# Expert weights in six places of 2 MiB, with neighbouring rows in each partition

## The chip, the cores and the metric

The kernel runs on one core of a Trainium2 chip. The metric is the device time of one execution in microseconds; lower is better. Engines are named as in the profile: PE is TensorE, DVE VectorE, ACT ScalarE, POOL GpSimd and SP SyncE, which here only issues DMAs.

## The reference

One layer of a hybrid decoder over 256 prompt tokens and 8 sample tokens. A token mixer (Mamba-2 branch, attention branch, output product) is followed by a layer norm, a mixture of 32 experts of which each token takes four, and a second norm. All weights are float32. The change concerns the experts alone:

```python
def run_block(args):
    tok_b, g_b, e = args
    h = xpad[tok_b] @ w_gate_up[e] + b_gate_up[e]        # 1024 -> 2048
    gate, up = h[:, :D_FF], h[:, D_FF:]
    gate = jnp.minimum(gate, SWIGLU_LIMIT)
    up = jnp.clip(up, -SWIGLU_LIMIT, SWIGLU_LIMIT)
    hmid = (up + 1.0) * (gate * jax.nn.sigmoid(SWIGLU_ALPHA * gate))
    out = hmid @ w_down[e] + b_down[e]                   # 1024 -> 1024
    return out * g_b[:, None].astype(out.dtype)
```

Every expert has 8 MiB of gate-up weights (1024 rows of 2048 floats, 8 KB a row) and 4 MiB of down weights (1024 rows of 1024 floats, 4 KB a row), 384 MiB for the 32.

## The kernel before

Up to about 460 us the token mixer runs; w_out follows until about 505 us, then the router, which ends at about 520 us. The expert stage takes the rest. It goes block by block, a block being up to 64 rows that go to one expert. With these inputs there are 32 blocks, one for each expert.

The order of a block on PE is written out by hand in the loop at L2097: gate_up(b) (L2035), down(b-1) (L2047), gather(b+1) (L2024), combine(b-1) (L2069), gate_rows(b) (L2062). Gather takes the block's rows of x1 with one-hot columns. Gate_up multiplies them, as the stationary operand in tiles of 128x32, with the weights as the moving operand: four matmuls of 512 columns (q = 0 to 3) run at the same time in four column groups of the array, and each of them goes through the array twice since the data is float32. DVE turns the result in blocks of 32x32 (L1545), adds the bias, clips, and makes hst (L1564), the stationary operand of down in the block after. Down has its result in bank 2 in two halves that run at the same time.

Weights come by DMAs of SP, 1 MiB each. A gate-up chunk is 128 neighbouring rows, one row of 8 KB in each partition (L468): partition p holds row p of the chunk. A down chunk is 256 rows, two of them of 4 KB in each partition, 128 rows apart (L472). The chunks rotate through 12 places (moe_slot, L330), made of tensors that earlier stages have left: whm, wmh, wmx and five of wnat; chunk 0 has a place of its own that is used once (EARLY). PE increments chunk_used after each chunk, and SP waits for the release of a place before it issues the next load into it: 20 loads are written out at L478 to L494, then block_chunks (L496) makes 12 a block, eight of gate-up and four of down of the block before. So SP's queue is always limited by releases, and as many chunks as are free are in flight. Of these 20, the ninth waits for branch_b (its place holds w_out_attn), the tenth to twelfth for one release of w_out each, the thirteenth for mix_psum. Behind that wait SP also issues the last six pieces of the copy of the key and value caches (move_cache, L364, DRAM to DRAM, about 1 MB each).

The places of columns matter for the change. The moving operand of gate-up is read as `w[:, q, u, k, i]` of columns (u k q i), 32 neighbouring floats at a time (L2040). Gather reads x1 as (k q i) in the same way (L2030).

## Time and profile before

| | |
|---|---|
| Time, median of three runs | 1500.97 us (1499.21 to 1502.39) |
| The profiled execution's own time | 1498.68 us |
| Its span, first to last instruction | 1497.0 us |
| PE busy | 1351.9 us (90%) |
| DVE, ACT, POOL busy | 596.1, 298.1, 164.8 us |
| DMA moved | 539.26 MB, mean 360 GB/s |

The profile is of one execution. Times in it are counted from the span's start. Busy time of PE is modelled for the ends of matmuls, and matmuls overlap. A timeline row can merge several instructions (x8 at its end says how many), so its duration is from the first start to the last end. The share of the DMA engines can stand a little above 1, since packets overlap.

### The profile page before, as it was taken

How to read it: one execution, taken by the hardware profiler on the slowest of the kernel's cores; microseconds unless marked ns; L12 is line 12 of the kernel's file. 1: busy time of each engine (PE TensorE's matmuls, PEld its weight loads, DVE VectorE, ACT ScalarE, POOL GpSimd, SP SyncE). 2: the span in 40 equal slices, each digit the busy share in tenths (PEclk: the TensorE clock that was granted, in tenths of full speed). 3: DMA queues.
4: the chain of work that ended last, by engine and by line, in shares of the span. 5: the costliest groups of instructions: out<-in, count | busy, mean ns of one | idle time of the engine just before them, and what ended most of it. 6: DMA issues, size and time to landing. Idle time of an engine off the chain costs nothing.

```text
span 1497.0 us, 25740 instructions
## 1 busy us (share of the span) xinstructions
PE 1351.9 (90%) x10344; PEld 675.9 (45%) x10344; DVE 596.1 (40%) x899; ACT 298.1 (20%) x603; POOL 164.8 (11%) x219
## 2 busy tenths in 40 slices
PE   5998997988999799999999999999998999899984
PEld 4997887986675433333222222223222322232221
DVE  2886999967544523222212121222122212221224
ACT  3677654454130100000000000000000000000002
POOL 0004455230300000000000000000000000000002
PEclk9999998998799899999999999999999999999998
DMA  6699999969468989999999999999999999999993
GB/s 192 196 365 322 297 326 327 326 225 326 151 234 324 328 329 419 417 416 419 419 417 416 419 418 418 416 418 418 418 416 418 418 419 415 418 418 419 416 416 120
DMA packets 164655, 539.26 MB, mean 360 GB/s; under 512 B 11036, under 2 KB 90236, under 8 KB 130996
## 3 DMA queue, kind: packets, MB, share of 16 engines
q1 hardware_dynamic: 152768, 523.57, 90.0%
q10 hardware_dynamic: 10692, 10.91, 2.6%
q0 software_dynamic: 1152, 4.20, 0.8%
q8 instruction: 29, 0.48, 0.1%
q14 instruction: 14, 0.11, 0.0%
HBM read 522.39 MB, written 60.43 MB: 389 GB/s over the span
## 4 chain that ended last, share of the span: by engine, by line
PE 34%; SPq 28%; DMA 22%; DVE 8%; issue 5%; ACT 2%; POOL 1%; ACTq 0%; DVEq 0%; POOLq 0%
SPq L472 17%; DMA wmx<-in_w_down_dram 12%; SPq L468 11%; DMA wmh<-in_w_down_dram 9%; PE psum L2043 6%; PE psum L1813 4%; PE psum L2058 4%; PE psum L1632 3%; PE psum L1633 3%; PE psum L1634 3%; PE psum L1951 2%; DVE wlow L1052 2%; PE psum L2031 1%; PE psum L2077 1%; DMA gn_rows<-in_ssm_norm_g_dram 1%
## 5 line engine op out<-in xcount | busy, mean ns | idle before, releaser
L2043 PE MATMUL psum<-wnat,xst 128*32 128x512 f32 x2480 | 272.5, 593 | 0.4 <-DVE xst L1511 0.4
L1545 DVE STREAM_TRANSPOSE hturn<-psum 128x1024 f32<-128x1024 f32 x32 | 40.0, 1250 | 404.6 <-PE psum L2043 404.6
L1632 PE MATMUL psum<-xh,wh 128*128 128x264 f32 x592 | 177.6, 300 | 6.3 <-DVE wlow L1052 5.3
L1634 PE MATMUL psum<-xh,wlow 128*128 128x264 f32 x592 | 171.3, 289 | 0.0
L1633 PE MATMUL psum<-xl,wh 128*128 128x264 f32 x592 | 171.3, 289 | 0.0
L2043 PEld LDWEIGHTS psum<-wnat,xst 128*32 128x32 f32 x2480 | 77.5, 110 | 172.6 <-issue 172.6
L2058 PE MATMUL psum<-wmx,hst 128*64 128x512 f32 x496 | 118.7, 603 | 31.9 <-DMA wmx<-in_w_down_dram 31.9
L2058 PE MATMUL psum<-wmh,hst 128*64 128x512 f32 x496 | 119.0, 602 | 30.0 <-DMA wmh<-in_w_down_dram 30.0
L992 ACT ACTIVATE sg<-hb 128x512 f32<-128x512 f32 x32 | 20.2, 631 | 526.5 <-DVE hb L1553 526.5
L1632 PEld LDWEIGHTS psum<-xh,wh 128*128 128x128 f32 x592 | 115.8, 196 | 9.4 <-issue 6.3
L2043 PE MATMUL psum<-wmh,xst 128*32 128x512 f32 x1056 | 119.2, 592 | 0.0
L1052 DVE TENSOR_TENSOR wlow<-wraw,wh 128x1024 fp32r<-128x1024 f32 x74 | 109.3, 1492 | 21.6 <-ACT wh L688 21.6
L1633 PEld LDWEIGHTS psum<-xl,wh 128*128 128x128 f32 x592 | 115.6, 195 | 1.7 <-issue 1.7
L1634 PEld LDWEIGHTS psum<-xh,wlow 128*128 128x128 f32 x592 | 115.0, 194 | 0.0
L628 POOL COPY gcol<-gm 128x3 f32 (+1 forms) x32 | 17.0, 533 | 849.3 <-DVE hb L1548 848.3
L2031 PE MATMUL psum<-x,oneh 128*32 128x256 f32 x1584 | 93.8, 386 | 3.1 <-DVE oneh L1495 3.1
L1564 DVE TENSOR_TENSOR hst<-hu,sg 128x512 f32<-128x512 f32 x32 | 22.1, 692 | 160.3 <-PE psum L2058 160.3
L2058 PEld LDWEIGHTS psum<-wmh,hst 128*64 128x64 f32 x496 | 32.8, 136 | 116.7 <-issue 79.9
L2058 PEld LDWEIGHTS psum<-wmx,hst 128*64 128x64 f32 x496 | 31.0, 136 | 118.8 <-DMA wmx<-in_w_down_dram 78.2
L688 ACT ACTIVATE wh<-wraw 128x1024 fp32r<-128x1024 f32 x74 | 77.7, 1052 | 0.0
L2031 PEld LDWEIGHTS psum<-x,oneh 128*32 128x32 f32 x1584 | 48.5, 111 | 58.6 <-issue 27.6
L1813 PE MATMUL psum<-zz,wnat 128*128 128x264 f32 x256 | 69.6, 431 | 3.5 <-DVE gates L1299 3.5
(390 smaller groups left out, 1477.7 us busy)
## 6 DMA issues: line engine op xcount, KB each, us to landing
wnat<-in_w_gate_up_dram SPq DMA_DIRECT2D x155, 1024.0 KB, 20.1
wmh<-in_w_gate_up_dram SPq DMA_DIRECT2D x66, 1024.0 KB, 24.1
wmh<-in_w_down_dram SPq DMA_DIRECT2D x62, 1024.0 KB, 26.2
wmx<-in_w_down_dram SPq DMA_DIRECT2D x62, 1024.0 KB, 23.3
wraw<-in_w_in_dram SPq DMA_DIRECT2D x37, 1024.0 KB, 8.9
whm<-in_w_gate_up_dram SPq DMA_DIRECT2D x33, 1024.0 KB, 22.3
out_dram<-in_cache_kv_w_dram SPq DMA_DIRECT2D x32, 1023.5 KB, 8.6
out_dram<-hs SPq DMA_DIRECT2D x8, 1024.0 KB, 11.9
```

The costliest lines, as they stand in the source:

```text
L468: sp.dma_start(moe_slot(m), wgu[bass.ds(e, 1), k * P:(k + 1) * P, :].rearrange("a p n -> p (a n)")).then_inc(moe_sem(m), 16)
L472: sp.dma_start(moe_slot(m).rearrange("p (a n) -> p a n", a=2), wdn[bass.ds(e, 1), j * 256:(j + 1) * 256, :].rearrange("e (a p) n -> p (e a ...
L688: a.activation(high_of(m), half_of(wraw, m), ACT.Copy).then_inc(S("high_done"), 1)
L1052: v.tensor_tensor(half_of(wlow, m), half_of(wraw, m), high_of(m).bitcast(F32), ALU.subtract).then_inc(S("low_done"), 1)
L1545: v.transpose(hturn[:, :], psum[:, 0:2, :].rearrange("p h c -> p (h c)")).then_inc(S("hidden_out"), 1)
L1632: mm(out, hi[:, k, :], xh[:, k, :], start=(k == 0), stop=False)
L1633: mm(out, hi[:, k, :], xl[:, k, :], start=False, stop=False)
L1634: last = mm(out, lo[:, k, :], xh[:, k, :], start=False, stop=(k == KT - 1))
L1813: last = mm(bank[6 + odd][:, 0:T], w[:, k, odd * P:(odd + 1) * P], zz[:, KT * (r // 2) + k, :], start=(r == 0 and k == 0), stop=(r == 3 an ...
L2031: last = mm(bank[0][q * QW:(q + 1) * QW, 256 * h:256 * h + 256], oneh[:, t, h * QW:(h + 1) * QW], src, start=(t == 0), stop=(t == 2))
L2043: last = mm(bank[h][q * QW:(q + 1) * QW, :], xst[:, h, k, :], w[:, q, :, :, :], start=(k == 0), stop=(k == GU_CH - 1))
L2058: last = mm(bank[2][BLK * half:BLK * half + BLK, :], hst[:, k, :, :].rearrange("p h r -> p (h r)"), w[:, col:col + 512], start=(k == 0), s ...
```

## The change

Chunks are 2 MiB, and there are six places of 2 MiB in the same tensors; the fifth place of wnat and the place of chunk 0 that was used once are joined or left. GU_CH is 4 and DN_CH 2, so a block has six chunks (PAIR). In a gate-up chunk partition p now holds the two neighbouring rows 2p and 2p+1 of 256 (16 KB), in a down chunk the four rows 4p to 4p+3 of 512 (16 KB).

Since the rows of the product lie otherwise over the partitions, the contraction's order changes in three other places to match: gather reads every second float of x1 (L2030), gate-up takes its columns with a step of four floats (L2040), so that the hidden values come out in the order in which down's rows lie, and the turn of the bias rows reads every fourth (L1611). Counts of chunk_used that others wait for are halved. The six cache copies stand before the fifth load instead of the thirteenth, and the last down chunk comes as two DMAs of 1 MiB with semaphores of their own (moe_last), of which each has 8 KB in a partition.

```diff
--- before.py
+++ after.py
@@ -53,9 +53,9 @@
 N_PROJ = 37
 N_SSM, N_ATT, N_OUT = 8, 1, 4
 HSN = 2
-GU_CH, DN_CH = 8, 4
-SLOTS = 12
-EARLY = 1
+GU_CH, DN_CH = 4, 2
+SLOTS = 6
+PAIR = GU_CH + DN_CH
 NQ, QW = 4, 32
 
 
@@ -329,30 +329,20 @@
 
         def moe_slot(m):
 
-            if m < EARLY:
-                return whm[:, 0, :]
-            at = (m - EARLY) % SLOTS
-            if at == 0:
-                return whm[:, 1, :]
-            if at < 5:
-                return wmh[:, at - 1, :]
-            if at < 7:
-                return wmx[:, at - 5, :]
-            return wnat[:, at - 7, :]
+            at = m % SLOTS
+            two = (whm[:, 0:2, :], wmh[:, 0:2, :], wmh[:, 2:4, :], wmx[:, :, :], wnat[:, 0:2, :], wnat[:, 2:4, :])[at]
+            return two.rearrange("p a n -> p (a n)")
 
         def moe_sem(m):
-            return S(f"moe_first{m}") if m < EARLY else S(f"moe_in{(m - EARLY) % SLOTS}")
+            return S(f"moe_in{m % SLOTS}")
 
         def moe_landed(eng, m, rep=0):
 
-            if m < EARLY:
-                eng.wait_ge(moe_sem(m), 16)
-            else:
-                eng.wait_ge(moe_sem(m), 16 * ((m - EARLY) // SLOTS + 1) + 16 * rep)
+            eng.wait_ge(moe_sem(m), 16 * (m // SLOTS + 1) + 16 * rep)
 
         def gate_up_done(eng, b):
 
-            eng.wait_ge(S("chunk_used"), 8 if isinstance(b, int) and b == 0 else 12 * b + 4)
+            eng.wait_ge(S("chunk_used"), GU_CH if isinstance(b, int) and b == 0 else PAIR * b + 2)
 
         block = keep.enter_context(nc.Block())
 
@@ -464,42 +454,42 @@
                 native(i)
                 move_cache(next(pieces))
 
-            def gate_up(m, e, k):
-                sp.dma_start(moe_slot(m), wgu[bass.ds(e, 1), k * P:(k + 1) * P, :].rearrange("a p n -> p (a n)")).then_inc(
-                    moe_sem(m), 16)
+            def gate_up(m, e, j):
+
+                sp.dma_start(moe_slot(m), wgu[bass.ds(e, 1), j * 256:(j + 1) * 256, :].rearrange(
+                    "e (p a) n -> p (e a n)", a=2)).then_inc(moe_sem(m), 16)
 
             def down(m, e, j):
-                sp.dma_start(moe_slot(m).rearrange("p (a n) -> p a n", a=2),
-                             wdn[bass.ds(e, 1), j * 256:(j + 1) * 256, :].rearrange("e (a p) n -> p (e a) n", p=P)).then_inc(
-                    moe_sem(m), 16)
+
+                sp.dma_start(moe_slot(m), wdn[bass.ds(e, 1), j * 512:(j + 1) * 512, :].rearrange(
+                    "e (p a) n -> p (e a n)", a=4)).then_inc(moe_sem(m), 16)
 
             sp.wait_ge(S("oT_ready"), 3)
             sp.wait_ge(S("kv_out"), 16 * 12)
-            for m in range(20):
-                if m == 8:
-                    sp.wait_ge(S("branch_b"), KT // 2)
-                elif 9 <= m < 12:
-                    sp.wait_ge(S("native_used"), N_SSM + m - 8)
-                elif m == 12:
-                    sp.wait_ge(S("mix_psum"), 3)
+            for m in range(10):
+                if m == 4:
                     for piece in pieces:
                         move_cache(piece)
-                elif m > 12:
+                    sp.wait_ge(S("branch_b"), KT // 2)
+                    sp.wait_ge(S("native_used"), N_SSM + 1)
+                elif m == 5:
+                    sp.wait_ge(S("native_used"), N_SSM + 3)
+                elif m > 5:
                     sp.wait_ge(S("chunk_used"), m - SLOTS + 1)
-                if m < 8:
+                if m < 4:
                     gate_up(m, 0, m)
-                elif m < 16:
-                    gate_up(m, 1, m - 8)
+                elif m < 8:
+                    gate_up(m, 1, m - 4)
                 else:
-                    down(m, 0, m - 16)
+                    down(m, 0, m - 8)
 
             def block_chunks(b, e, e_before):
-                for c in range(12):
-                    sp.wait_ge(S("chunk_used"), 12 * b + c - 15)
+                for c in range(PAIR):
+                    sp.wait_ge(S("chunk_used"), PAIR * b + c - 7)
                     if c < GU_CH:
-                        gate_up(c + 8, e, c)
+                        gate_up(c + 4, e, c)
                     else:
-                        down(c + 8, e_before, c - GU_CH)
+                        down(c + 4, e_before, c - GU_CH)
 
 
             with sp.Fori(2, NE) as b:
@@ -515,9 +505,13 @@
                     block_chunks(b, e, before)
             last = sp.value_load(tab[0:1, bass.ds(nblk - 1, 1)], min_val=0, max_val=NE - 1)
             extra = sp.value_load(tab[0:1, MAX_BLK + 4:MAX_BLK + 5], min_val=0, max_val=MAX_OV)
-            for j in range(DN_CH):
-                sp.wait_ge(S("chunk_used"), 12 * extra + 12 * NE + j - 15)
-                down(j + 8, last, j)
+            sp.wait_ge(S("chunk_used"), PAIR * extra + PAIR * NE - 7)
+            down(4, last, 0)
+            sp.wait_ge(S("chunk_used"), PAIR * extra + PAIR * NE - 6)
+            quarter = moe_slot(5).rearrange("p (a n) -> p a n", a=4)
+            for i in range(2):
+                sp.dma_start(quarter[:, 2 * i:2 * i + 2, :], wdn[bass.ds(last, 1), 512:1024, :].rearrange(
+                    "e (p a) n -> p (e a) n", a=4)[:, 2 * i:2 * i + 2, :]).then_inc(S(f"moe_last{i}"), 16)
             for t in range(2):
                 for half in range(2):
                     cols = slice(512 * half, 512 * half + 512)
@@ -994,7 +988,7 @@
 
             def expert_rows(b):
 
-                act.wait_ge(S("chunk_used"), 12 * b + 20)
+                act.wait_ge(S("chunk_used"), PAIR * b + 10)
                 a.activation(orow[:, :], bank[2], ACT.Copy).then_inc(S("orow_ready"), 1)
 
             def gate_rows(b):
@@ -1010,7 +1004,7 @@
                 sigmoid(b)
                 expert_rows(b - 1)
                 gate_rows(b)
-            act.wait_ge(S("chunk_used"), 12 * nblk)
+            act.wait_ge(S("chunk_used"), PAIR * nblk)
             a.activation(orow[:, :], bank[2], ACT.Copy).then_inc(S("orow_ready"), 1)
 
 
@@ -1576,7 +1570,7 @@
                 gated(b)
                 one_hot(b + 1)
                 hidden(b)
-                dve.wait_ge(S("chunk_used"), 12 * b + 8)
+                dve.wait_ge(S("chunk_used"), PAIR * b + 4)
                 hidden_in(b)
                 rows_in(b + 1)
 
@@ -1608,7 +1602,9 @@
                 i, o = divmod(f, 12)
                 tr(bank[i][:, 32 * o:32 * o + 29], rows[:, f * P:(f + 1) * P], ident[0:29, 0:29])
             for f in range(2 * KT):
-                tr(bank[2][:, NE * f:NE * f + NE], bgu_rows[:, f * P:(f + 1) * P], ident[0:NE, 0:NE])
+                u, j, c = f // KT, f % KT // 4, f % 4
+                of_four = bgu_rows[:, :].rearrange("e (u j i c) -> e u j c i", u=2, j=2, c=4)
+                tr(bank[2][:, NE * f:NE * f + NE], of_four[:, u, j, c, :], ident[0:NE, 0:NE])
             tr(bank[3][:, 0:ZT], gn_rows[:, :], ident[0:ZT, 0:ZT]).then_inc(stage("params_psum"), 1)
 
             pe.wait_ge(S("x_in"), 32)
@@ -2027,7 +2023,7 @@
                 for h in range(2):
                     for t in range(3):
                         for q in range(NQ):
-                            src = x1[:, t, :].rearrange("p (k q i) -> p q k i", q=NQ, i=QW)[:, q, :, :]
+                            src = x1[:, t, :].rearrange("p (j q i a) -> p q j a i", q=NQ, i=QW, a=2)[:, q, :, :, :]
                             last = mm(bank[0][q * QW:(q + 1) * QW, 256 * h:256 * h + 256], oneh[:, t, h * QW:(h + 1) * QW],
                                       src, start=(t == 0), stop=(t == 2))
                 last.then_inc(S("gath_done"), 1)
@@ -2035,26 +2031,32 @@
             def gate_up(b, m0, rep):
 
                 pe.wait_ge(S("xst_ready"), b + 1)
-                for k in range(GU_CH):
-                    moe_landed(pe, m0 + k, rep)
-                    w = moe_slot(m0 + k).rearrange("p (u k q i) -> p q u k i", u=2, q=NQ, i=QW)
-                    for h in range(2):
-                        for q in range(NQ):
-                            last = mm(bank[h][q * QW:(q + 1) * QW, :], xst[:, h, k, :], w[:, q, :, :, :], start=(k == 0),
-                                      stop=(k == GU_CH - 1))
+                for j in range(GU_CH):
+                    moe_landed(pe, m0 + j, rep)
+                    w = moe_slot(m0 + j).rearrange("p (a u j q i c) -> p a q u j c i", a=2, u=2, j=2, q=NQ, i=QW)
+                    for a_ in range(2):
+                        k = 2 * j + a_
+                        for h in range(2):
+                            for q in range(NQ):
+                                last = mm(bank[h][q * QW:(q + 1) * QW, :], xst[:, h, k, :], w[:, a_, q, :, :, :, :],
+                                          start=(k == 0), stop=(k == KT - 1))
                     last.then_inc(S("chunk_used"), 1)
 
-            def down(b, m0, rep):
+            def down(b, m0, rep, final=False):
 
                 pe.wait_ge(S("hst_ready"), b + 1)
                 pe.wait_ge(S("gt_ready"), b + 1)
                 for j in range(DN_CH):
-                    moe_landed(pe, m0 + j, rep)
+                    in_halves = final and j == DN_CH - 1
+                    if not in_halves:
+                        moe_landed(pe, m0 + j, rep)
                     w = moe_slot(m0 + j)
-                    for a_ in range(2):
-                        k = 2 * j + a_
+                    for c in range(4):
+                        if in_halves and c % 2 == 0:
+                            pe.wait_ge(S(f"moe_last{c // 2}"), 16)
+                        k = 4 * j + c
                         for half in range(2):
-                            col = a_ * D + 512 * half
+                            col = c * D + 512 * half
                             last = mm(bank[2][BLK * half:BLK * half + BLK, :], hst[:, k, :, :].rearrange("p h r -> p (h r)"),
                                       w[:, col:col + 512], start=(k == 0), stop=(k == KT - 1))
                     last.then_inc(S("chunk_used"), 1)
@@ -2095,13 +2097,13 @@
             gather(1)
             gate_rows(0)
             with pe.Fori(1, nblk) as b:
-                gate_up(b, 8, b - 1)
-                down(b - 1, 16, b - 1)
+                gate_up(b, 4, b - 1)
+                down(b - 1, 8, b - 1)
                 pe.wait_ge(S("hidden_out"), b + 1)
                 gather(b + 1)
                 combine(b - 1, False)
                 gate_rows(b)
-            down(nblk - 1, 8, nblk - 1)
+            down(nblk - 1, 4, nblk - 1, final=True)
             combine(nblk - 1, True)
```

## Rows read from the trace of the kernel before

**Rows 1.** The page: DMA share and rate in 40 slices.

```profile
DMA  6699999969468989999999999999999999999993
GB/s 192 196 365 322 297 326 327 326 225 326 151 234 324 328 329 419 417 416 419 419 417 416 419 418 418 416 418 418 418 416 418 418 419 415 418 418 419 416 416 120
```

**Rows 2.** SP's issues in order of time (start us, us, queue, line).

```profile
698.10 1.03 SPq L468 DMA_DIRECT2D whm<-in_w_gate_up_dram  x1
...
1421.23 1.02 SPq L468 DMA_DIRECT2D whm<-in_w_gate_up_dram  x1
```

**Rows 3.** The same view, first issues of two early blocks.

```profile
551.32 7.18 SPq L468 DMA_DIRECT2D wnat<-in_w_gate_up_dram  x5
...
578.33 7.19 SPq L468 DMA_DIRECT2D wnat<-in_w_gate_up_dram  x5
```

**Rows 4.** One block in order of time; idle before in brackets.

```profile
999.97 1.94 PE L2058 MATMUL psum<-wmh,hst 128*64 128x512 f32 x8 [0.63 <-DMA wmh<-in_w_down_dram]
...
1007.54 1.94 PE L2058 MATMUL psum<-wmx,hst 128*64 128x512 f32 x8 [0.60 <-DMA wmx<-in_w_down_dram]
1009.41 2.80 PE L2031 MATMUL psum<-x,oneh 128*32 128x256 f32 x48
...
1015.53 8.79 PE L2043 MATMUL psum<-wnat,xst 128*32 128x512 f32 x80
...
1021.14 0.13 PEld L2043 LDWEIGHTS psum<-wnat,xst 128*32 128x32 f32 x4 [0.30 <-issue]
1021.57 0.13 PEld L2043 LDWEIGHTS psum<-wnat,xst 128*32 128x32 f32 x4 [0.30 <-issue]
...
1029.54 1.25 DVE L1545 STREAM_TRANSPOSE hturn<-psum 128x1024 f32<-128x1024 f32 x1 [12.72 <-PE psum L2043]
```

**Rows 5.** DMA view of windows 1028:1034, 1008:1024 and 1038:1054 us.

```profile
DMA packets 637, 2.45 MB, mean 408 GB/s; under 512 B 39, under 2 KB 39, under 8 KB 637
...
DMA packets 928, 6.75 MB, mean 422 GB/s; under 512 B 104, under 2 KB 104, under 8 KB 104
...
DMA packets 924, 6.72 MB, mean 420 GB/s; under 512 B 104, under 2 KB 104, under 8 KB 104
```

**Rows 6.** First blocks, and one window (PE, PEld, DVE, ACT, POOL, clock, DMA).

```profile
526.01 3.64 PE L2043 MATMUL psum<-whm,xst 128*32 128x512 f32 x32 [0.41 <-DVE xst L1511]
...
539.88 3.69 PE L2017 MATMUL psum<-bdn,gmT 32*128 32x512 f32 x8
...
549.19 8.79 PE L2043 MATMUL psum<-wnat,xst 128*32 128x512 f32 x80 [0.45 <-DVE xst L1511]
...
550.00:552.50 2.50, 2.50 (x28) 0.81 (x24) 0.00 (x0) 0.00 (x0) 0.00 (x0) 1.00 0.25 64
```

**Rows 7.** The end in order of time.

```profile
1459.46 1.94 PE L2058 MATMUL psum<-wmx,hst 128*64 128x512 f32 x8 [0.61 <-DMA wmx<-in_w_down_dram]
...
1461.33 2.80 PE L2031 MATMUL psum<-x,oneh 128*32 128x256 f32 x48
...
1468.42 7.09 PE L2058 MATMUL psum<-wnat,hst 128*64 128x512 f32 x32 [0.90 <-ACT gsam L1005]
```

**Rows 8.** Bias rows turned, and the issue of six cache copies.

```profile
15.94 1.89 PE L1611 MATMUL psum<-ident,bgu_rows 32*128 32x32 f32 x16
...
504.37 3.72 SPq L373 DMA_DIRECT2D out_dram<-in_cache_kv_w_dram  x6
```

**Rows 9.** Five DVE lines: count, min/median/max ns, first and last start.

```profile
L1502 DVE TENSOR_TENSOR pick<-pick,gate x1: 557/557/557, 521.3 to 521.3; 128x384 f32<-128x384 f32 x1
...
L1506 DVE TENSOR_REDUCE gm<-pick x1: 834/834/834, 521.9 to 521.9; 128x96 f32<-128x384 f32 x1
...
L1464 DVE TENSOR_REDUCE mask<-pick x3: 363/369/375, 511.6 to 515.3; 128x32 f32<-128x128 f32 x2, 8x32 f32<-8x128 f32 x1
...
L1263 DVE TENSOR_REDUCE ast<-pa x12: 285/286/287, 346.2 to 371.6; 128x1 f32<-128x128 f32 x12
...
L1264 DVE TENSOR_REDUCE ast<-pa x12: 407/408/409, 346.4 to 371.8; 128x1 f32<-128x256 f32 x12
```

## The prediction

> **What bounds the kernel now.** I read the page first, then the DMA's own view in short windows, then the order of time of one expert block, of the first blocks and of the end. [rows 1] is the page: in the 16th slice and after (about 561 us) the sixteen DMA engines are busy in every slice at 415 to 420 GB/s, and in the table above TensorE is busy nine tenths of the span. Both look like the bound, so the pace of each is needed by itself. [rows 2] gives the pace at which weights arrive: SP's issue of the same place falls at 698.10 and, 24 blocks later, at 1421.23, so a block takes 723.13 / 24 = 30.13 us. A block is 12 MiB, so 2.511 us a MiB. [rows 3] gives TensorE's own pace: at 551 and 578 us all places are full, TensorE waits for nothing, and SP's issues (each follows a release by TensorE) lie 27.01 us apart. TensorE therefore has 30.13 - 27.01 = 3.12 us of slack in a block. [rows 4] shows where it lies: in one block the first and the fourth down chunk start at 999.97 and 1007.54, so 2.52 us lie between two of them, and each is held up 0.6 us by its DMA; the gate-up run from 1015.53 to about 1029.3 is one piece of 13.7 us. The stage is bound by the arrival of weights, and everything that shortens a transfer counts about 30 times.
>
> **Packet size.** In [rows 5] the first window holds almost only packets of 4 KB (the down chunks, rows of 1024 floats; the count under 8 KB is all of it) and moves 408 GB/s; the other two hold packets of 8 KB (gate-up, rows of 2048 floats) and move 422 and 420. The small packets counted there are the completions. The same two places of other blocks spread by 2 GB/s about their means, and I take 410 and 422 GB/s: 1.0486 MB takes 2.557 and 2.485 us. Doubling the packet from 4 to 8 KB saved 0.072 us a MiB. If the cost is one fixed amount for each packet, going on to 16 KB halves the remaining count and saves half of that again, 0.036: 2.449 us a MiB, 428 GB/s. A block of six places then takes 12 x 2.449 = 29.39 us instead of 30.13. Bounds: nothing gained beyond 8 KB gives 2.485 (29.82 a block, the down chunks still gain); no packet cost at all left would be 2.485 - 0.072 = 2.413 (28.96 a block). I take the middle value, since a fixed cost a packet is the simplest reading of the two kinds of window.
> The Trainium skill (DMA: Bandwidth & Descriptors, Why small descriptors are slow) says that each packet has a fixed overhead of about 3 cycles, and (Bandwidth, Measured) that a 16 MB transfer ran at 425 GB/s. By the latter a block would take 29.6 us, close to the sum. The trace agrees in sign: 410 against 422.
>
> **How many blocks it counts for.** In [rows 6] TensorE starts gate-up of block 0 at 526.01, ends it at 539.88, and is back at 549.19. By then it has released 8 MiB, 12 more are loaded, and the DMA runs dry: share 0.25 at 550.0 to 552.5. It resumes after the first release (SP's issue at 551.32) with 20 of 384 MiB loaded. The last four are needed only by the very last down. So 384 - 20 - 4 = 360 MiB stand between the restart and the chunk that lets the tail begin: 360 x (2.511 - 2.449) = 22.3 us gained, bounds 9.4 (2.485) and 35.3 (2.413).
>
> **Coarser places, at the restart.** A place of 2 MiB is released after 3.43 us of matmuls instead of 1.71 (13.7 us for eight chunks, [rows 4]). The DMA is dry at that moment, so the restart is 1.7 us later. The four places released in block 0 are issued from 529.5 on and take 4.9 us each after some 2 us of latency, so the last of them lands at about 551.1, just before the new first release at 549.19 + 3.43 = 552.6: as many MiB are loaded as before. Cost 1.7 us.
>
> **Coarser places, in a steady block.** After the last down chunk of 2 MiB lands (call it 0), TensorE needs 3.55 us for it, 6.05 for gather, combine and gate rows (1009.48 to 1015.53, [rows 4]) and 13.75 for gate-up: 23.4, with 0.6 before the next down. The next gate-up places land at 4.9, 9.8, 14.7 and 19.6, each before it is wanted; the down places at 24.5 and 29.4. The first is done at 28.1, 1.3 us before the second lands. Nothing is lost, with 1.3 us of cover within a block and 29.39 - 27.01 = 2.4 us over it. The queue doesn't run dry either: the unread backlog at the start of gate-up is at most 10 us of transfer, two places, one more is being read, so at least three of six are in flight. TensorE starts 12 MiB (29 us) behind and gains 2.4 us a block, so it has caught up after some twelve of 31 blocks.
>
> **Coarser places, at the end.** In [rows 7] the last down chunk of the loop starts at 1459.46, right after landing, and what follows never waits for a transfer: gather at 1461.33, down of the last block from 1468.42 for 7.09 us, then the norm and the outputs to 1497. With 2 MiB the same run of down takes 3.5 us after its landing instead of 1.9: 1.6 us later. The split of the very last place into two halves buys nothing here, since TensorE reaches it about 3 us after both have landed; it costs nothing either.
>
> **The cache copies.** The six copies left over, now issued behind mix_psum at 504.37 in 3.72 us ([rows 8]), move ahead of the fifth place on SP. Places 5 and 6 queue behind them. They wait for the first and third release of w_out and so are issued before 504.4, when the last one lets the copies go today. Six copies and 4 MiB take under 30 us together, and the places are wanted only at 549. Nothing on SP behind them is due earlier. The very first places are issued at 464 to 468.6 as before. What of SP's waits goes (half of them) was no cost: SP waits for releases. Cost 0, covered by some 15 us or more; without that cover the copies would cost their own time, about 12 us (six times 1 MB read and written at 420 GB/s and twice that at most). The permuted bias transposes read their stationary operand with a step; the 16 of them span 1.9 us ([rows 8]), so even doubled they cost 1.9 us. I take 0.
>
> **The step in the moving operand.** Now the matmuls of gate-up read weights in runs of 32 neighbouring floats; afterwards every fourth float (16 bytes apart), and gather every second of x1. No TensorE row of before has such an operand, so this is bounded. Low end 0. The nearest rows are VectorE's [rows 9]: 384 floats in runs take 557 ns (L1502), a reduction that reads 384 floats with a step of 32 takes 834 (L1506), 1.50 times; between 128 and 384 stepped floats the slope is (834 - 369) / 256 = 1.82 ns, against (408 - 286) / 128 = 0.95 in runs (L1263, L1264): 1.9 times. Applied to the 13.75 us of gate-up that is 6.9 or 12.6 us a block. I take 0, because TensorE takes 512 columns in 0.43 us, 0.83 ns for a float of one stream ([rows 4], four streams at once), already only a little faster than VectorE's 0.95, and its pace is set by float32 arithmetic in two passes and not by the first access; this is the weakest step.
>
> **Sum.** Span 1497.0 - 22.3 + 1.7 + 1.6 = 1478.0. The profiled execution took 1498.68, 1.7 over its span and 2.3 under the median of the three runs, 1500.97. On the median: 1500.97 - 19.0 = 1482.
>
> **Rivals.**
> (a) Larger packets bring nothing beyond 8 KB: 1500.97 - 9.4 + 3.3 = 1494.9. For it: two kinds of packet are all that the trace shows. Against: the gain from 4 to 8 KB is plain. Chance 0.10.
> (b) Slower: the step in the weights slows gate-up. It decides from 2.4 us a block, 17% of gate-up's time; below 1.3 it costs nothing. At 1.50 times a block is 27.0 + 6.9 = 33.9 us of TensorE: block 0 ends at 549.2 + 6.9 = 556.1, 31 blocks to 1607, tail 29.5, 1636 of span, about 1640. At 1.9 times it is 39.6 a block, about 1823. For it: [rows 9], and that four streams share the reading side at once, where they could hurt each other more than one. Against: nothing in the trace but the pace above. Chance 0.20 for a slowdown of this kind. The Trainium skill (SBUF — State Buffer, Door 1, on cachelines) has the rule behind it: lines are 16 bytes, at least two accesses must fall in one for full rate, and four float32 are as far as a step is free. Here each line would give one float. By [rows 9] VectorE agrees; no TensorE row can say.
> (c) A small slowdown, 2.4 to 3.2 us a block, from gather's step of two or the same cause: TensorE is the bound at 29.4 to 30.2 us and the time is within some 3 us of the present. Chance 0.05.
> (d) Six places are too few: with one read and one partly filled the DMA idles 0.3 to 1 us a block. 30 x that: 1491 to 1512. Against: the backlog worked out above leaves three in flight. Chance 0.05, most of it slower.
>
> **How the numbers follow.** Forecast 0.60; (a) 0.10, (b) 0.20, (c) 0.05, (d) 0.05. 0.2% is 3 us, about what a measurement of this kernel can tell from no change. Faster: 0.60 + 0.10 = 0.70; same: (c) and a part of (d), 0.07; slower: 0.23. The range leaves out (b) and reaches from near the best packet price (1469, taken as 1472) to the end of (d), 1512.
>
> **What would show it.** Windows of packets of 16 KB at about 428 GB/s, the same place issued every 29.4 us; gate-up still one run of 13.7 us and gather 2.8; TensorE waiting for DMA only ahead of down; a DMA share of 1 from about 557 on; the tail from the last down of the loop 1.6 us longer. Wrong if gate-up's run is over 16 us, or if rows of TensorE show no waits for DMA late in the stage: then (b) or (c). Wrong the other way if the windows still show 422.

## The result, and the profile after

| | before | after |
|---|---|---|
| Time, median (lowest to highest) | 1500.82 us (1499.21 to 1502.39) | 1915.24 us (1910.46 to 1917.26) |
| Span of the profiled execution | 1497.0 us | 1914.9 us |

The change makes the kernel slower by the factor 1.2757, with a 95% interval of 1.2728 to 1.2785. The forecast was 1482 with a range of 1472 to 1512. The time lies far outside it, on the side of rival (b).

The page of after, the parts that answer to [rows 1], with PE's busy time, the chain and the costliest line, and below them the chain of before:

```profile
PE 1824.9 (95%) x10344; PEld 707.5 (37%) x10344; DVE 595.5 (31%) x899; ACT 298.0 (16%) x603; POOL 164.5 (9%) x219
...
DMA  6899997767746777777867777787777778777770
GB/s 193 295 339 311 331 323 260 242 231 285 281 176 264 281 296 299 301 292 312 314 270 303 291 293 300 303 314 299 274 299 303 293 292 314 313 278 293 292 291 23
...
PE 90%; DVE 5%; issue 2%; ACT 1%; DMA 1%; POOL 1%; another core or an unknown queue 1%; ACTq 0%; DVEq 0%; POOLq 0%
...
L2041 PE MATMUL psum<-wnat,xst 128*32 128x512 f32 x1984 | 453.6, 1081 | 0.5 <-DVE xst L1505 0.5
```

```profile
PE 34%; SPq 28%; DMA 22%; DVE 8%; issue 5%; ACT 2%; POOL 1%; ACTq 0%; DVEq 0%; POOLq 0%
```

In the expert stage the DMA engines now have seven to eight tenths of their time busy and move about 300 GB/s where 415 to 420 stood. The chain of work that ended last, followed back from the end, is now nine tenths PE; before, half of it was SP's queue and its transfers. A gate-up matmul takes 1081 ns where the page of before has 593, and the granted clock is 1.00 from 600 to 1880 us, so it is not the clock. So the stage has changed its bound: before it waited for weights, now the weights wait.

One block of after in order of time, which answers to [rows 4], then two passes of gate-up's weight loads, then SP's issue of the same place in two blocks, which answers to [rows 2]:

```profile
1026.16 3.65 PE L2060 MATMUL psum<-wmh,hst 128*64 128x512 f32 x16
1029.65 3.60 PE L2060 MATMUL psum<-wmx,hst 128*64 128x512 f32 x16
1033.18 2.94 PE L2027 MATMUL psum<-x,oneh 128*32 128x256 f32 x48
...
1039.45 14.68 PE L2041 MATMUL psum<-wnat,xst 128*32 128x512 f32 x64
...
1068.51 1.94 PE L2060 MATMUL psum<-wmh,hst 128*64 128x512 f32 x8
```

```profile
1044.84 0.15 PEld L2041 LDWEIGHTS psum<-wnat,xst 128*32 128x32 f32 x4 [0.75 <-issue]
1045.74 0.15 PEld L2041 LDWEIGHTS psum<-wnat,xst 128*32 128x32 f32 x4 [0.75 <-issue]
```

```profile
1019.22 0.33 SPq L459 DMA_DIRECT2D whm<-in_w_gate_up_dram  x1
...
1061.52 0.33 SPq L459 DMA_DIRECT2D whm<-in_w_gate_up_dram  x1
```

No row has a wait for a DMA in its brackets. Gate-up runs from 1039.45 to the first down matmul at 1068.51, 29.1 us instead of 13.75; a pass of four matmuls takes 0.90 us instead of 0.43 [rows 4]. Down and combine are as they were. A block takes 42.30 us, and that is 27.01 [rows 3] + 32 passes x 0.47 = 15.04 + 0.14 for gather (2.94 instead of 2.80) = 42.19.

The span grew by 417.9 us. Block 0 starts at 530.90 instead of 526.01: 4.9. From there to the second block's gate-up (574.31) it is 43.41 us instead of 23.18: 20.2, of which gate-up is 15.3 and a lower clock behind it 4.8 (run 6). From the second block to the start of the last block's down (1886.36; before 1468.42, [rows 7]) it is 1312.05 instead of 919.23 us, 31 blocks of 42.3: 392.8. The tail after that is as long as before (28.5 and 28.6).

The first 4.9 us have a cause of their own, which the row of PE's one new wait names:

```profile
511.71 0.66 PE L1964 MATMUL psum<-xres,wr 128*32 128x128 f32 x8 [10.95 <-DMA bdn<-in_b_down_dram]
```

The router's logits wait 10.95 us for a load of 128 KB on ACT's queue, the experts' down bias. It lands 53.7 us after its issue, in the kernel before 27.0. From the end of w_out to block 0 it is 30.2 us here and 21.7 before, 8.5 more; the start moved by 4.9 only because w_out ended 3.6 us earlier in this execution (500.69 against 504.27).

### The profile page after: what moved, and what is told of

Same layout as the page of the kernel before. It is cut to its first block, busy times and chain, and to the rows that moved or that the text cites. A ratio compares the mean times of both kernels' runs of the same rounds, so it can differ in the third digit from the quotient of the medians.

```text
span 1914.9 us, 25006 instructions
## 1 busy us (share of the span) xinstructions
PE 1824.9 (95%) x10344; PEld 707.5 (37%) x10344; DVE 595.5 (31%) x899; ACT 298.0 (16%) x603; POOL 164.5 (9%) x219
## 4 chain that ended last, share of the span: by engine, by line
PE 90%; DVE 5%; issue 2%; ACT 1%; DMA 1%; POOL 1%; another core or an unknown queue 1%; ACTq 0%; DVEq 0%; POOLq 0%
PE psum L2041 48%; PE psum L2060 12%; PE psum L2027 5%; PE psum L1809 3%; PE psum L2079 3%; PE psum L1628 3%; PE psum L1629 3%; PE psum L1630 3%; PE psum L2084 2%; PE psum L1947 1%; DVE wlow L1046 1%; PE psum L2068 1%; DMA wnat<-in_w_out_dram 0%; DMA gn_rows<-in_ssm_norm_g_dram 0%
## 5 line engine op out<-in xcount | busy, mean ns | idle before, releaser
L2041 PE MATMUL psum<-wnat,xst 128*32 128x512 f32 x1984 | 453.6, 1081 | 0.5 <-DVE xst L1505 0.5
L2041 PE MATMUL psum<-wmh,xst 128*32 128x512 f32 x1056 | 245.3, 1083 | 0.0
L2041 PE MATMUL psum<-whm,xst 128*32 128x512 f32 x1024 | 237.4, 1080 | 0.4 <-DVE xst L1505 0.4
L2041 PEld LDWEIGHTS psum<-wnat,xst 128*32 128x32 f32 x1984 | 71.8, 126 | 329.9 <-issue 329.9
L986 ACT ACTIVATE sg<-hb 128x512 f32<-128x512 f32 x32 | 20.2, 631 | 1010.9 <-DVE hb L1547 1010.9
L2041 PEld LDWEIGHTS psum<-wmh,xst 128*32 128x32 f32 x1056 | 41.8, 129 | 196.7 <-issue 196.7
L2060 PE MATMUL psum<-wmh,hst 128*64 128x512 f32 x496 | 113.3, 599 | 0.0
L2060 PE MATMUL psum<-wmx,hst 128*64 128x512 f32 x496 | 111.7, 592 | 0.0
L2041 PEld LDWEIGHTS psum<-whm,xst 128*32 128x32 f32 x1024 | 41.2, 129 | 188.6 <-issue 188.1
L2027 PE MATMUL psum<-x,oneh 128*32 128x256 f32 x1584 | 101.2, 404 | 3.1 <-DVE oneh L1489 3.1
```

The source lines that it names most:

```text
L2027: last = mm(bank[0][q * QW:(q + 1) * QW, 256 * h:256 * h + 256], oneh[:, t, h * QW:(h + 1) * QW], src, start=(t == 0), stop=(t == 2))
L2041: last = mm(bank[h][q * QW:(q + 1) * QW, :], xst[:, h, k, :], w[:, a_, q, :, :, :, :], start=(k == 0), stop=(k == KT - 1))
L2060: last = mm(bank[2][BLK * half:BLK * half + BLK, :], hst[:, k, :, :].rearrange("p h r -> p (h r)"), w[:, col:col + 512], start=(k == 0), s ...
```

## The experiments

Three questions: is it the step of four in gate-up, and nothing else (runs 1 and 2)? What in the step costs (3 and 4)? What is the rest of the change worth (5 to 11)? The kernel before ran beside them on each chip, at 1496.5 to 1497.1 us.

**1. The step of four alone, in the kernel before.**

```diff
-  w = moe_slot(m0 + k).rearrange("p (u k q i) -> p q u k i", u=2, q=NQ, i=QW)
+  w = moe_slot(m0 + k).rearrange("p (u j q i c) -> p q u j c i", u=2, j=2, q=NQ, i=QW)
```

> The kernel before with one part of the change alone: gate-up reads its moving operand with a step of four floats; loads, places, copies and gather stay. The hidden values then stand in another order than the rows of down, so the experts' output is another one. Theory: gate-up takes 32 passes of 0.90 us, 28.8 instead of 13.7 us, TensorE is the bound at 27.0 + 15.1 = 42.1 us a block, 549.2 + 15.1 + 31 x 42.1 + 29.5 gives a span of about 1899, near 1900 us. Rival: the slowdown needs the transfers of 16 KB beside it; then the time stays near 1497 us.

Measured 1900.76 us, ratio 1.2696 (1.266 to 1.2732). SP's issues of one place, eight blocks apart:

```profile
797.91 0.33 SPq L468 DMA_DIRECT2D whm<-in_w_gate_up_dram  x1
...
1134.49 0.33 SPq L468 DMA_DIRECT2D whm<-in_w_gate_up_dram  x1
```

336.58 / 8 = 42.07 us a block. This one line carries 404 of the 414 us. The rest of the change, which was to save 19 us, costs some here: the span of after is 15.6 us longer than that of this run (1914.9 against 1899.3), since block 0 starts 8.7 us later and each of 31 blocks takes 0.23 us more, of which gather's step of two is 0.14. Cheaper transfers bring nothing while PE is the bound.

**2. All of the change without that step.**

```diff
-  w = moe_slot(m0 + j).rearrange("p (a u j q i c) -> p a q u j c i", a=2, u=2, j=2, q=NQ, i=QW)
+  w = moe_slot(m0 + j).rearrange("p (a u k q i) -> p a q u k i", a=2, u=2, q=NQ, i=QW)
```

> The changed kernel with one thing undone: gate-up reads its moving operand in runs of 32 neighbouring floats again. The hidden values then stand in another order than the rows of down, so the experts' output is another one; loads, places, gather with its step of two and every count of instructions are those of the changed kernel. Theory: the step of four floats in gate-up's moving operand is the whole loss, and the rest of the change does what the prediction said. Then four matmuls take 0.43 us again instead of 0.90, a block is bound by its transfers at 29.4 us, and the time is 1482 us (1475 to 1490). Rival 1: the coarse places or gather's step lose too; then a block takes over 30 us and the time is above 1500. Rival 2: matmuls are slow since the transfers of 16 KB disturb the reading side; then 0.90 us stays and the time is near 1915.

Measured 1487.0 us, ratio 0.9936 (0.9915 to 0.9956). SP's issues of the place whm, 23 blocks apart:

```profile
731.97 0.33 SPq L459 DMA_DIRECT2D whm<-in_w_gate_up_dram  x1
...
1408.15 0.33 SPq L459 DMA_DIRECT2D whm<-in_w_gate_up_dram  x1
```

676.18 / 23 = 29.40 us a block, where the prediction had worked out 29.39. The kernel before beside it had 1496.47, so it gains 9.5 us where the prediction's sum had 19.0 for all but the step. The wait at the logits is here too (9.8 us), and runs 7 to 11 are about it.

**3. Eight patterns of the moving operand in one gate-up.** In the kernel before, each of the eight chunks is read in another way; all matmuls have 512 columns.

```diff
+  if k == 0:
+      return flat[:, 512 * q:512 * q + 512]
+  if k == 1:
+      return flat[:, 128 * q:128 * q + 1024].rearrange("p (x s) -> p x s", s=2)[:, :, 0]
+  if k == 2:
+      return flat[:, 128 * q:128 * q + 1536].rearrange("p (x s) -> p x s", s=3)[:, :, 0]
+  if k == 3:
+      return flat.rearrange("p (x s) -> p x s", s=4)[:, :, q]
+  if k == 4:
+      return flat.rearrange("p (q i c) -> p q c i", q=NQ, c=4)[:, q, :, :]
...
+  return flat.rearrange("p (q i b c) -> p q b i c", q=NQ, b=2, c=2)[:, q, :, :, :]
```

> The kernel before with another read pattern in each of the eight gate-up chunks, each 512 floats a stream, four streams at once; the output is not the reference's, only the spacing of the groups of four matmuls is read. Chunks in order: one run of 512; step 2; step 3; step 4 with the four streams on the same 16 bytes; step 4 with streams apart; step 8; step 32; pairs of neighbours with a step of 4 from pair to pair. Theory A (the four streams share a reading side that serves one 16-byte line at a time): 0.43 us for the run, the time of a pass is the larger of 0.43 and the number of line changes (2048 at a step of 4 or more) times 0.44 ns, so step 2 and the pairs 0.45, step 3 0.68, step 4, 8 and 32 0.90; streams on the same lines, if the side can hand one line to all, 0.43, else 0.90. Theory B (each stream pays for each change of line, 1.76 ns): step 4, 8, 32 0.90 as well, step 3 between 0.43 and 0.90, pairs 0.43 to 0.66, same lines 0.90. Theory C (cost by distance, such as banks): step 8 or 32 differs from step 4.

The weight loads of one gate-up, two neighbouring passes of a pattern at a time: a run of 512, step 2, step 3, step 4 (streams apart), step 32, pairs.

```profile
1022.77 0.13 PEld L2060 LDWEIGHTS psum<-wnat,xst 128*32 128x32 f32 x4 [0.30 <-issue]
1023.20 0.13 PEld L2060 LDWEIGHTS psum<-wnat,xst 128*32 128x32 f32 x4 [0.30 <-issue]
...
1024.96 0.13 PEld L2060 LDWEIGHTS psum<-wnat,xst 128*32 128x32 f32 x4 [0.32 <-issue]
1025.41 0.13 PEld L2060 LDWEIGHTS psum<-wnat,xst 128*32 128x32 f32 x4 [0.32 <-issue]
...
1027.20 0.14 PEld L2060 LDWEIGHTS psum<-wnat,xst 128*32 128x32 f32 x4 [0.54 <-issue]
1027.88 0.14 PEld L2060 LDWEIGHTS psum<-wnat,xst 128*32 128x32 f32 x4 [0.54 <-issue]
...
1033.07 0.14 PEld L2060 LDWEIGHTS psum<-wnat,xst 128*32 128x32 f32 x4 [0.76 <-issue]
1033.97 0.14 PEld L2060 LDWEIGHTS psum<-wnat,xst 128*32 128x32 f32 x4 [0.76 <-issue]
...
1041.18 0.16 PEld L2060 LDWEIGHTS psum<-wmh,xst 128*32 128x32 f32 x4 [0.70 <-issue]
1042.04 0.16 PEld L2060 LDWEIGHTS psum<-wmh,xst 128*32 128x32 f32 x4 [0.70 <-issue]
...
1043.40 0.12 PEld L2060 LDWEIGHTS psum<-wmh,xst 128*32 128x32 f32 x4 [0.34 <-issue]
1043.86 0.13 PEld L2060 LDWEIGHTS psum<-wmh,xst 128*32 128x32 f32 x4 [0.34 <-issue]
```

A load starts when the pass before its own does, so the distance of two neighbours is the time of a pass: 0.43, 0.45, 0.68, 0.90, 0.86 and 0.46 us; step 4 with all streams on the same 16 bytes is 0.90 as well, step 8 0.92. Pairs step over 16 bytes too and cost almost nothing. What counts is how many of its floats lie in each piece of 16 bytes: two or four are nearly free, one costs 2.1 times, and a step of three, where 512 floats lie in 384 pieces, lies between. All patterns write the same columns of PSUM, and the granted clock is 1.00.

**4. The number of streams.** Two chunks keep four column groups; the others use one, two, three or four of them, in runs or with a step of four. A group's matmuls then follow each other.

```diff
+  plan = ((4, 1), (1, 1), (2, 1), (1, 4), (2, 4), (3, 4), (4, 4), (4, 1))
+  groups, step = plan[k]
...
+  for n in range(3 if groups == 3 else 4):
+      q = n % groups
```

> The kernel before with another number of column groups at once in each gate-up chunk; the output is not the reference's. Chunks in order: 4 groups in runs, 1 group in runs, 2 groups in runs, 1 group at step 4, 2 groups at step 4, 3 groups at step 4 (three matmuls instead of four), 4 groups at step 4, 4 groups in runs. Theory A (shared reading side): one and two streams at step 4 take no longer than in runs (one pass 0.43 us: four matmuls of one stream 1.7 us, of two 0.86), three 0.68 and four 0.90 a pass of all. Theory B (each stream pays): every pass at step 4 takes 0.90 however many there are (one stream 3.6 us for four, two 1.8, three and four 0.90).

One stream in runs, and one stream with a step of four:

```profile
1032.36 0.11 PEld L2047 LDWEIGHTS psum<-wnat,xst 128*32 128x32 f32 x1 [0.32 <-issue]
1032.79 0.11 PEld L2047 LDWEIGHTS psum<-wnat,xst 128*32 128x32 f32 x1 [0.32 <-issue]
...
1044.95 0.13 PEld L2047 LDWEIGHTS psum<-wnat,xst 128*32 128x32 f32 x1 [0.77 <-issue]
1045.86 0.13 PEld L2047 LDWEIGHTS psum<-wnat,xst 128*32 128x32 f32 x1 [0.77 <-issue]
```

0.43 and 0.90 us for one matmul by itself, the same as for four at once. So the streams don't share a reader that the step would overload; each stream alone reads at 1.76 ns a float (0.90 us / 512) when each piece of 16 bytes gives it one. That is near VectorE's 1.82 ns from [rows 9], which was at a step of 32; TensorE takes 1.68 there (0.86 us, run 3). Whether both have the same cause no run shows.

**5. A kernel that computes the reference without the step in gate-up.** Gate-up reads runs of 128 columns, so a hidden value lies in the other order in PSUM, and DVE's turn of the result reads that with a step of four instead.

```diff
-  v.transpose(hturn[:, :], psum[:, 0:2, :].rearrange("p h c -> p (h c)"))
+  v.transpose(hturn[:, :].rearrange("p (g c i) -> p g c i", c=4, i=QW),
+              psum[:, 0:2, :].rearrange("p h (g i c) -> p (h g) c i", i=QW, c=4))
```

> All of the changed kernel, with the step moved from TensorE to VectorE: gate-up reads runs of 128 neighbouring floats, so the columns in PSUM stand in the order of the hidden values, and the transpose of 32x32 blocks that follows (1.25 us in both kernels) reads them from PSUM with a step of four. It computes what the reference computes. Theory: TensorE at 0.43 us for four matmuls, 29.4 us a block, 1482 us. VectorE's transpose may double to 2.5 us; VectorE waits 5.7 us for down after it, so nothing of it shows before the last block, at most 1.3 us. Rival: a transpose that reads with a step costs several times as much (over 7 us); then hst comes late and a block takes longer than 30 us.

Measured 1486.55 us, ratio 0.9925 (0.9904 to 0.9946), and on another chip 1486.1 (run 11): 9.9 us under the kernel before, nearly as run 2. The turn takes 1.25 us as in [rows 4], although it steps by four floats through PSUM:

```profile
1028.40 1.25 DVE L1539 STREAM_TRANSPOSE hturn<-psum 128x1024 f32<-128x1024 f32 x1 [12.72 <-PE psum L2042]
```

**6. Step two and packets of 8 KB, in the kernel before.** A down chunk gives each partition two neighbouring rows; gate-up then needs a step of two.

```diff
-  sp.dma_start(moe_slot(m).rearrange("p (a n) -> p a n", a=2),
-               wdn[bass.ds(e, 1), j * 256:(j + 1) * 256, :].rearrange("e (a p) n -> p (e a) n", p=P)).then_inc(
+  sp.dma_start(moe_slot(m), wdn[bass.ds(e, 1), j * 256:(j + 1) * 256, :].rearrange(
+      "e (p a) n -> p (e a n)", a=2)).then_inc(moe_sem(m), 16)
```

> The kernel before with a smaller version of the change: the 12 places of 1 MiB stay and the copies too, only a down chunk holds two neighbouring rows in each partition (8 KB packets instead of 4 KB), and gate-up reads its moving operand with a step of two floats, 8 bytes, to match. It computes what the reference computes. Theory (two floats used of each 16 bytes cost nothing): four matmuls take 0.43 to 0.45 us, a block takes 12 x 2.485 = 29.8 instead of 30.13 us, 30 blocks give 9 us: 1487 to 1488 beside 1496.5. Rival: a step of two costs TensorE more than the 2.8 us of slack it has in a block; then the time is above 1497.

Measured 1494.6 us, ratio 0.9968 (0.9952 to 0.9984). The steady block is as expected (issues of one place at 937.47 and, eight blocks later, 1176.44: 29.87 us), but the time is not. Block 0, and the columns of one window (busy PE, PEld, DVE, ACT, POOL, the granted clock, DMA share, GB/s):

```profile
543.50 1.97 PE L2020 MATMUL psum<-zero 128*64 128x512 f32 x2
545.40 1.88 PE L2022 MATMUL psum<-bdn,gmT 32*8 32x512 f32 x4
547.21 4.30 PE L2032 MATMUL psum<-x,oneh 128*32 128x256 f32 x48
...
552.44 3.86 PE L2044 MATMUL psum<-wnat,xst 128*32 128x512 f32 x32 [0.46 <-DVE xst L1510]
```

```profile
544.00:551.00 7.00, 7.00 (x50) 2.00 (x52) 1.16 (x2) 0.00 (x0) 0.52 (x1) 0.55 0.69 289
```

The granted clock stands at 0.55, near the lower of its two levels (1.2 GHz), after some 19 us of gate-up and bias matmuls without a pause. In the kernel before PE is as busy from 526.01 to 548.7 us, and the clock stays at 1.00. The same four bias matmuls take 1.03 us in the kernel before. From block 0 to the second it is 27.40 us instead of 23.18 [rows 6], 3.3 of the 4.2 us from the clock.

> The same kernel as before_pairs, for a second profile. Its steady block was as worked out (29.87 us), yet the time was 1494.6 where 1487 to 1488 was expected; in its profile TensorE had a granted clock of 0.87 between 525 and 552 us (before: 1.00) and block 0 took 27.4 us instead of 23.2. If that low clock is a matter of that execution, this profile shows 1.00 there, block 0 takes 23.2 us and the span is near 1489. If it shows 0.87 again, the clock belongs to the kernel's own order of work and the time stays at about 1494.

On the second chip: 1488.88 us, ratio 0.9951 (0.9926 to 0.9977). The clock of 0.87 between 525 and 552 us and block 0 of 27.3 us came again in its profile, which was of one of its longest executions (1494.94, where the shortest took 1485.69). So the fall is no single accident of one execution, and the same is seen in after (0.59 between 561 and 572 us) and in run 1 (0.50 between 557 and 564 us). Which executions have it can't be read from times alone; why the kernels with runs don't show it stays open.

**7. All of the change but the step in gate-up, and the cache copies back in their old place.** This is the kernel of run 5 with one more edit.

```diff
                 if m == 4:
-                    for piece in pieces:
-                        move_cache(piece)
...
                 elif m > 5:
+                    if m == 6:
+                        sp.wait_ge(S("mix_psum"), 3)
+                        for piece in pieces:
+                            move_cache(piece)
```

> The changed kernel with VectorE's transpose taking the step of four (as in turn_steps) and with the six cache copies put back behind the wait for mix_psum, ahead of the seventh load. It computes what the reference computes. In the runs so far bdn, a load of ACT's queue issued before the copies, landed 52.5 us after its issue with the copies early and 27.0 us with them late, and TensorE stood 9.5 us before the router's logits for it. Theory: the early copies cost the start of the stage some 7 us; undone, gate-up of block 0 starts at about 526 again, and the time is 7 us below turn_steps, about 1479 beside 1496.5 for the kernel before. Rival: the start is late by the six new transfers of 2 MiB with 16 KB packets themselves; then TensorE still waits for bdn and the time stays at 1486.

Measured 1478.21 us, ratio 0.9886 (0.9863 to 0.9909): 1.1% faster than the kernel before. The rows that answer to [rows 2] and [rows 7]:

```profile
694.01 0.33 SPq L459 DMA_DIRECT2D whm<-in_w_gate_up_dram  x1
...
1399.17 0.33 SPq L459 DMA_DIRECT2D whm<-in_w_gate_up_dram  x1
```

```profile
1437.40 3.65 PE L2063 MATMUL psum<-wmx,hst 128*64 128x512 f32 x16 [1.16 <-DMA wmx<-in_w_down_dram]
...
1448.23 7.09 PE L2063 MATMUL psum<-wnat,hst 128*64 128x512 f32 x32 [0.90 <-ACT gsam L1001]
```

**8. The copies early, alone.** In the kernel before, the six copies stand before the ninth load, so behind 8 MiB of places as in the change.

> The kernel before with one part of the change alone: the six cache copies stand ahead of the ninth load (with the change: ahead of the fifth) instead of behind mix_psum. It computes what the reference computes. Theory: they take the DMA engines while bdn is on its way; TensorE waits for bdn before the logits, the stage starts some 7 us later, and the time is 5 to 8 us above the kernel before. Rival: with eight loads ahead of them the copies come late enough to be harmless, or the restart absorbs it; within 2 us of the kernel before.

Measured 1496.66 us, ratio 1.0001 (0.9985 to 1.0017): nothing. The bias lands 26.1 us after its issue, and PE does not wait for it.

**9. A semaphore of its own for the bias load.**

```diff
-  act.dma_start(bdn[:, :], b_down[0]).then_inc(S("router_in"), 16)
+  act.dma_start(bdn[:, :], b_down[0]).then_inc(S("bdn_in"), 16)
```

> The kernel of turn_steps (all of the change, cache copies early, gate-up reading runs of 128 and VectorE reading its PSUM with a step), and only this besides: the load of the experts' down bias, 128 KB on ACT's queue, signals a semaphore of its own, which TensorE awaits at the bias matmuls (about 540 us), and the router's logits and VectorE wait for the other two router loads alone (32 instead of 48). Nothing else moves; the copies stay ahead of the fifth place. In the trace of turn_steps the bias lands 52.5 us after its issue at 459.9, so at 512.4, and TensorE stands 9.5 us at the logits; the router's own loads land at 25.3 and 32.1 us, so by 492. Theory C (the early copies cost time only through this one wait): no wait of TensorE for a DMA at the logits, block 0 starts at 524 to 526 instead of 532.3, the span is 7 us under turn_steps, about 1478 against 1496.7 of the kernel before, ratio 0.988, though the bias still lands over 50 us after its issue. Rival D (the copies also hold up the fifth and sixth place or another load that the stage start needs): a new wait takes its place and block 0 still starts after 529; 1483 to 1487, ratio 0.991 to 0.994.

Measured 1479.33 us, ratio 0.9884 (0.9859 to 0.9909). The time is that of theory C, its mechanism is not. Start of the logits:

```profile
506.68 1.26 PE L1965 MATMUL psum<-xres,wr 128*32 128x128 f32 x32 [7.61 <-DMA br<-in_b_router_dram]
```

The wait went over to br, which lands 52.3 us after its issue here and 32.1 in run 5. Between the end of w_out's last eight matmuls (499.0) and block 0 (525.77) lie 26.8 us; in run 5 it is 29.4, before 21.7. Only 2.6 us are the semaphore's. The rest of the gain in this profile comes from w_out, which ended 3.9 us earlier than in run 5, and nothing in the edit explains that. Over all these profiles w_out ends between 497.7 and 504.6 us, and in runs 5 and 11, one kernel, at 502.9 and 500.4, so a single profile can't price it.

**10. The router's loads first on ACT's queue.**

```diff
+  act.dma_start(wr[:, :, :], w_router[0].rearrange("(k p) e -> p k e", p=P)).then_inc(S("router_in"), 16)
+  act.dma_start(br[:, :], b_router.broadcast_to([P, NE])).then_inc(S("router_in"), 16)
+  act.dma_start(bdn[:, :], b_down[0]).then_inc(S("router_in"), 16)
   act.dma_start(xres[:, 0:2, :], x_prompt[0].rearrange("(t p) d -> p t d", p=P)).then_inc(S("xres_in"), 16)
...
```

> The kernel of turn_steps (cache copies early) with one edit: the three loads of the router (wr, br, bdn) are issued on ACT's queue ahead of the residual rows and the layer norm's rows instead of behind them. In turn_own_sem the wait at the router's logits did not go: it was 7.6 us, now for br, which landed 52.3 us after its issue there and 32.1 us in turn_steps; so what comes last on ACT's queue is held up behind the 2 MiB places and the copies, whichever load it is. If that is the whole cost of the early copies, the router's loads now land within some 20 us, TensorE does not wait for a DMA at the logits, and block 0 starts 21.7 to 22 us after the first matmul of the logits could start (the end of w_out's last eight matmuls), as in the kernel before and in turn_late_copies; in turn_steps it was 29.4 us and in turn_own_sem 26.8. Time 1478 to 1480. Rival: the residual or norm rows come late in their place, or the fifth and sixth place do, and the wait only changes its name: 1483 to 1487.

Measured 1482.62 us, ratio 0.9897 (0.9873 to 0.992). Logits and block 0:

```profile
504.61 0.75 PE L1965 MATMUL psum<-xres,wr 128*32 128x128 f32 x32
...
526.38 3.64 PE L2042 MATMUL psum<-whm,xst 128*32 128x512 f32 x32 [0.41 <-DVE xst L1505]
```

Now the wait is gone and the distance is 21.8 us, with the copies early. The three loads land 2.4 to 3.8 us after their issue. In the other kernels some 2 MB of residual and norm rows stand before them on ACT's own queue, so what the early copies cost hangs on that order as well. But PE waits 4.1 us for the last piece of w_out instead of 2.1: part of the gain is given back.

**11. Run 5 again, beside run 10.**

> The same kernel as turn_steps, beside turn_router_first on one chip and for a second profile. Expected 1486.5 again, a wait of 8 to 11 us for the router's loads, and block 0 about 29 us after the end of w_out's last eight matmuls. If the wait is much shorter here, its size is a matter of the execution and the 7 us between turn_steps and turn_late_copies are no firm price.

1486.1 us, ratio 0.9921 (0.9892 to 0.9949); a wait of 9.6 us, and 29.4 us again to block 0:

```profile
510.04 1.26 PE L1965 MATMUL psum<-xres,wr 128*32 128x128 f32 x32 [9.60 <-DMA bdn<-in_b_down_dram]
```

## Why the prediction was wrong, point by point

**The step that failed: the moving operand, taken at 0.** [rows 9] gave 1.5 to 1.9 times, and the prediction chose the low end by an argument: TensorE's pace is set by float32 arithmetic in two passes, not by the first access. Runs 3 and 4 refute it. The read costs 1.76 ns a float and TensorE takes 0.84, so the read is the bound as soon as a float comes alone. The argument had the very number that speaks against it: an engine that takes a float in 0.83 ns has no room for a read that costs VectorE 1.82. The nearest rows should have been taken, and with them rival (b) should have been the forecast. Rival (b)'s thought that four streams hurt each other more than one fell too (run 4). Its condition held: the slowdown decides from 2.4 us a block, and it is 15.1.

**Rival (b) was right in kind and too low.** 12.6 us a block were priced (1823); 15.1 were measured. The ratio of slopes, 1.9, was applied to TensorE's 13.75 us, but that time is shorter than VectorE's for the same floats. Had 1.82 ns been taken as the read's own time, 512 x 1.82 = 0.93 us a pass gives 16 us a block and about 1930. The Trainium skill (SBUF — State Buffer, Door 1, on cachelines) asks for at least two accesses in a line of 16 bytes for full rate. Runs 3 and 4 agree for TensorE reading float32: two in a line 0.45 us, one 0.90. The same passage has four float32 as the limit of a free step; here a step of four costs 2.1 times, so read as a step from float to float it does not hold for TensorE.

**Packet size: right.** Packets of 16 KB came at 428 GB/s (window 1000 to 1008 of run 7), a block at 29.38 to 29.40 us; predicted 428 and 29.39. A block all in packets of 8 KB took 29.87 us (run 6), so the step from 8 to 16 KB is real, and rival (a) falls.

**Restart, steady block, end: right.** In run 7 the stretch from the second block's start (547.60) to the last down of the loop (1437.40) takes 889.80 us, before 1459.46 - 549.19 = 910.27: -20.5, and the sum said -22.3 + 1.7. The rest of the span from there is 39.3 instead of 37.5 us: +1.8, and the sum said 1.6. The waits are 0.8 and 1.16 us ahead of the two down chunks, and the DMA share is 1.01 from 570 us on, so rival (d) falls.

**Gather's step of two: small, as rival (c) had it.** 2.94 instead of 2.80 us, 0.14 a block, covered while the weights are the bound. Where PE is the bound it costs its time (run 1). The permuted bias transposes took 2.08 instead of 1.89 us, so the 0 for them was fair.

**The cache copies: taken at 0, and wrong.** The cover was counted for SP's own queue (places 5 and 6) and held there. What was left out is ACT's queue: the router's small loads are in flight at the same time, and the last of them landed 25 us later (52.5 to 53.7 us after its issue in the profiles of after and of runs 2, 5 and 11, before 27.0). From the end of w_out to block 0 it is 29.4 us (runs 5 and 11) against 21.7; 7.6 us in the profile. In time it is less certain: run 7 against run 5 is 0.9886 against 0.9925, 6 us (8.6 by the medians, each less that of the kernel before beside it), and run 10 against run 11 on one chip 3.5. Neither part of the change does it alone: the copies behind loads of 1 MiB cost nothing (run 8), and packets of 16 KB with the copies late move the bias only to 30.0 us. The Trainium skill (DMA: Bandwidth & Descriptors, Queues, rings and completion order) says that each DMA engine goes round between the queues that have work, a packet at a time, so larger packets on SP's queue would keep ACT's small loads longer; the step from 27.0 to 30.0 us agrees in sign, the one to 52.5 is not explained by it. Ahead of all this traffic the same loads land within 4 us (run 10). Why they starve so much longer with 16 KB packets and the copies together was not settled, and run 9 shows that it can be another load than the one named by the wait in run 5.

**The whole sum.** -19.0 was predicted for the rest of the change, and run 7, which is that rest with the copies put back, is 18.5 under the kernel before beside it (1478.21 and 1496.72), by the ratio 17 (13.6 to 20.5). As the change stands, with the copies early, the same rest gave 9.5 to 11 us (runs 2, 5 and 11). The loss is one access pattern: 0.47 us x 32 passes x 32 blocks = 481 us, less the slack that had been there.

## What to carry to other kernels

Before a contraction order is permuted, look at the innermost step of every moving operand, and price it by the slowest read of the same step that any engine shows, not by how busy TensorE seems. Two neighbouring floats are enough; if an order must be broken up, break it up in the turn on VectorE that reads PSUM, which took 1.25 us either way for a step of four. And when copies are moved on one queue, look at the small loads on the others: the engine that waits may belong to them.

## What the runs showed of the hardware

- TensorE's pass of 512 float32 columns from SBUF takes 0.43 to 0.46 us (0.84 to 0.90 ns a float) if at least two of each 16 bytes are used, and 0.86 to 0.92 us (1.68 to 1.80 ns) if one is (run 3); the number of column groups at work (1 to 4) makes no difference (run 4).
- DVE's transpose of 128x1024 float32 in blocks of 32x32 reads PSUM with a step of four floats in the same 1.25 us as without (run 5).
- Packets of 4, 8 and 16 KB: about 410, 421 and 428 GB/s [rows 5], runs 6 and 7: 2.56, 2.49 and 2.45 us a MiB, as a fixed cost for each packet would give.
- A load of 128 KB on ACT's queue, behind some 2 MB of that queue, landed 52 to 54 us after its issue while 8 MiB in packets of 16 KB and six copies stood in SP's queue, after 30.0 without the copies, after 26.1 with the copies and packets of 8 KB, and after 3.2 when issued first of all (run 10).
- TensorE's granted clock fell to near 0.5 for some 7 to 10 us in block 0 after its gate-up, in kernels with a step of two or four there, and cost 3 to 5 us; in those with runs it stayed at 1.00. Why is open.
